# The first norm's root taken out of the input of a two-block transformer kernel and put into what reads the projections

## The chip, the cores and the metric

The kernel runs on one core of one Trainium2 chip. The metric is the device time of one execution in microseconds (us). Several executions of the kernel before gave 969.68, 969.88 and 971.83 us, median 969.88. One more execution was recorded by the hardware profiler; it took 969.85 us.

The engines are named as the profile names them: PE is TensorE (PEld its weight loads), DVE VectorE, ACT ScalarE, POOL GpSimd, SP SyncE, which only issues DMAs here.

## The reference, cut to what matters

Two transformer blocks over 256 tokens of width 1024, all in float32. The change touches only the first norm of the first block and the readers of its product:

```python
u = rms_norm(h, ln_pre_mix)          # h * rsqrt(mean(h*h) + eps) * gain, one root per token
proj = u @ w_in                      # 1024 x 9232
q_a, k_a, v_a, qkv_b, z_b, b_b, a_b, gate_a, gate_b = split(proj)
qa, ka = apply_rope(q_a, cos, sin), apply_rope(k_a, cos, sin)
y_a = attention(qa, ka, v_a)
qkv_b = silu(causal_depthwise_conv(qkv_b, conv_w))    # 4 taps along the tokens
... b_b, a_b -> rates of the gated delta rule; z_b -> silu(z); gate_a, gate_b -> sigmoid
```

The root of a token is one factor on its whole row of `proj`, so it can be applied to `u` before the product or to each part of `proj` after it.

## The kernel before, in words

**Weights.** All weights stream through one pipeline in units of 128 x 1024 floats (512 KB). SP issues the DMA of unit n into one of four raw buffers, once the low half of unit n-4 is made (L478 to L482). ACT rounds the unit to fp32r, the high half `w_hi` (`split_up_to`, L1320 to L1334), into one of six slots; unit n can be rounded only when PE has released the unit that held the slot before (`w_used`), so unit 6 needs unit 0 released. POOL computes the low half `w_lo = raw - w_hi` in two instructions of 128 x 512 per unit (L499 to L505). Each product is three fp32r matmuls: high x high, high x low, low x high. ACT's roundings stand in program order among its other work: at most so many units ahead as the calls of `split_up_to` name.

**The input, step `u`.** x lands in two halves of 128 tokens. ACT squares each half with a running sum; DVE makes the root of each in six one-element instructions (`rsqrt_one`); ACT and DVE scale the half by its root into `xn0`; PE transposes it (L947) in fp32 into the banks Q0 to Q3; ACT (odd banks) and DVE (even banks) evict with the gain of each channel as scale into `uH` (fp32r), and DVE then forms `uL = x*gain - uH`. Dummy matmuls (`warm`) keep PE busy until then. The transpose of the convolution taps and gains (`cwr`) is copied by DVE to `cw`.

**The first convolution group, `first_conv` (L900).** For each of the four units (0 to 3): eight matmuls high x high, eight with `uL`. Then for each unit eight matmuls with `w_lo`, at the end of each the unit is released. So the first unit is released only after the whole first part.

**Order after that.** Every engine walks the same list of steps: `u`, `conv 0 0`, `ba`, `conv 0 1`, `rates`, `tri 0`, `conv 0 2`, `decay 0`, (`moba 0 0` inside it), `tok 0` and so on; then a second group of heads with the same steps. For `conv`, DVE runs the taps from the banks: per tile of 128 channels one TENSOR_SCALAR and three SCALAR_TENSOR_TENSOR of 128 x 256, four tiles per step. `rates` is a chain of tiny instructions between DVE and ACT. `tri` gives the products `trg` (mask times decay rates), which PE needs in `decay` (L999). At the end of `decay` DVE adds the masks ("decay log", L2150). PE waits in `tok` for the banks read by the taps of `conv 0 2` (the filling step `moba 0 1` uses L0 and L1) and for the second "decay log" before it transposes into Q0 (L983). The columns of `moba`, `z`, `ga`, `gb` are filling steps: their matmuls stand between the latency-bound parts of PE's list.

**The root helpers.** `rsqrt_one` (L1933) works on one column; its other factors are pointer scalars, so no instruction has two tensor inputs. `rsqrt` (L1921) works on several columns: one TENSOR_SCALAR, then three rounds of three instructions, each with two tensor inputs. Its argument `bank` puts one of these tensors in PSUM; all calls before give it.

Of the kernel before, what the change touches and what calls it, by code (L numbers as in the profile page):

```python
# [22 lines left out]
F32 = mybir.dt.float32  # L23
# [196 lines left out]
def build(nc, a, out, known):  # L220
# [30 lines left out]
    with ctx:  # L251
# [20 lines left out]
        small = place("small", [P, 960])  # L272
# [106 lines left out]
        def tiny(n):  # L379
            free[0] += n  # L380
            assert free[0] <= 960
            return small[:, free[0] - n:free[0]]
# [37 lines left out]
        r1, floor = tiny(8), tiny(8)  # L420
        baH = big("baH", 36, [P, KD, 16], F32R)
# [90 lines left out]
        def _(pe):  # L512
# [387 lines left out]
            def first_conv():  # L900
# [3 lines left out]
                for j in range(4):  # L904
# [27 lines left out]
            for step in SCHEDULE:  # L932
                kind = step[0]
                if kind == "u":
                    n = CONV * 24 + KD
                    pe.wait_ge(*VE(step, "constant"))
                    warm(15)
                    pe.wait_ge(landed["ident"], 16)
                    pe.wait_ge(landed["cwr"], 16)
                    pe.wait_ge(landed["ln0"], 16)  # L940
                    turn(L[3][:, 0:n], cwr[0:n, :], ident[0:n, 0:n]).then_inc(*PE.mark(step, "taps"))
                    warm(5)
                    for t in range(NT):
                        for j in range(4):
                            pe.wait_ge(*(VE(step, "scaled", 1, j) if t == 1 and j < 2 else AC(step, "scaled", t, j // 2)))
                            for i in range(2):
                                last = turn(Q[j][:, i * SEQ + t * P:i * SEQ + (t + 1) * P], xn0[:, t, (2 * j + i) * P:(2 * j + i + 1) * P], ident)  # L947
                            if t == 1:
                                last.then_inc(*PE.mark(step, "turned", j))
                elif step in INSIDE:  # L950
# [363 lines left out]
        def _(act):  # L1314
# [154 lines left out]
            for step in SCHEDULE:  # L1469
# [5 lines left out]
                if kind == "u":  # L1475
# [7 lines left out]
                    load("table", table[:, P:], a["table"][:, P:])  # L1483
                    act.wait_ge(*VE(step, "root", 0))
                    for half in range(2):
                        cc = slice(half * 512, (half + 1) * 512)
# [1030 lines left out]
```

## Time and profile before

| | |
|---|---|
| median of 3 executions | 969.88 us |
| profiled execution | 969.85 us |
| its span, first to last instruction | 968.0 us |
| mean granted TensorE clock | 0.998 |
| PE busy | 958.0 us, 99% |
| POOL busy | 742.8 us, 77% |
| ACT busy | 511.5 us, 53% |
| DVE busy | 365.8 us, 38% |

The profiled execution's own time lies 1.85 us over its span. A share near 100% says that an engine is nearly always occupied; the share of the others is an average over stretches in which they wait and stretches in which they work without a gap, so the timeline of a stretch has to be read as well.

### The profile page before, as it was taken

The page shows a single profiled execution, that of the slowest core. Times are in us where ns is not written, and L with a number is a line of the kernel's source. Part 1 is how long each engine was busy: PE and PEld are TensorE (multiplying, and loading weights), DVE is VectorE, ACT ScalarE, POOL GpSimd, SP SyncE. Part 2 cuts the span into 40 slices and gives each one's busy share as a digit, 9 for nine tenths or more (in the row PEclk, how much of TensorE's full clock was granted, in tenths as well). Part 3 has the DMA queues.
Part 4 walks back from the last instruction along what each step waited for, and adds up shares of the span by engine and source line. Part 5 has one row for each costly group of instructions (what it writes and reads, how often), then busy time and mean ns, then how long its engine had stood idle before and what let it go on. Part 6 is the DMA issues. An engine that isn't in the chain of part 4 may idle for free.

```text
span 968.0 us, 14697 instructions
## 1 busy us (share of the span) xinstructions
PE 958.0 (99%) x5708; PEld 815.1 (84%) x5708; DVE 365.8 (38%) x844; ACT 511.5 (53%) x753; POOL 742.8 (77%) x593
## 2 busy tenths in 40 slices
PE   9999999999999999999999999999999999999997
PEld 8988879988878888888888887899888888888885
DVE  5687625785624245031122245052343241111103
ACT  6576635464644347455354556584566564444431
POOL 5967654876654988899877987778876889888890
PEclk9999999999999999999999999999999999999999
DMA  7746242654434766767644665656565557666541
GB/s 261 216 132 196 89 137 77 181 154 149 132 110 137 255 213 179 237 193 211 202 153 139 211 219 168 233 155 187 182 196 152 152 163 228 182 189 192 179 130 44
DMA packets 76750, 167.33 MB, mean 173 GB/s; under 512 B 8348, under 2 KB 13704, under 8 KB 76552
## 3 DMA queue, kind: packets, MB, share of 16 engines
q1 hardware_dynamic: 71296, 156.40, 53.3%
q10 hardware_dynamic: 5384, 9.99, 3.2%
q8 instruction: 45, 0.74, 0.3%
q14 instruction: 25, 0.20, 0.1%
HBM read 165.32 MB, written 1.05 MB: 172 GB/s over the span
## 4 chain that ended last, share of the span: by engine, by line
PE 97%; DVE 1%; ACT 1%; DMA 0%; issue 0%; DVEq 0%; ACTq 0%
PE L L517 23%; PE L L519 22%; PE L L518 22%; PE Q L519 2%; PE Q L517 2%; PE Q L518 2%; PE L L889 2%; PE L L891 2%; PE L L890 2%; PE Q L734 1%; PE Q L1185 1%; PE L L788 1%; PE L L790 1%; PE L L789 1%; PE Q L852 1%; PE L L827 1%
## 5 line engine op out<-in xcount | busy, mean ns | idle before, releaser
L504 POOL TENSOR_TENSOR w_lo<-raw,w_hi 128x512 fp32r<-128x512 f32 x588 | 741.3, 1299 | 201.7 <-ACT w_hi L1333 201.1
L1333 ACT CAST w_hi<-raw 128x1024 fp32r<-128x1024 f32 x294 | 305.2, 1055 | 244.1 <-PE L L519 106.2
L517 PE MATMUL L<-w_hi,uH 128*128 128x512 f32 (+1 forms) x768 | 305.4, 398 | 0.3
L519 PE MATMUL L<-w_hi,uL 128*128 128x512 f32 (+1 forms) x768 | 296.6, 386 | 0.0
L518 PE MATMUL L<-w_lo,uH 128*128 128x512 f32 (+1 forms) x768 | 296.1, 386 | 0.0
L519 PEld LDWEIGHTS L<-w_hi,uL 128*128 128x128 f32 x768 | 144.3, 188 | 29.8
L517 PEld LDWEIGHTS L<-w_hi,uH 128*128 128x128 f32 x768 | 144.5, 188 | 29.3 <-DVE uL L1949 1.5
L518 PEld LDWEIGHTS L<-w_lo,uH 128*128 128x128 f32 x768 | 144.7, 188 | 26.5 <-issue 0.5
L517 PE MATMUL L<-w_hi,hH 128*128 128x512 f32 x176 | 69.0, 392 | 0.0
L519 PE MATMUL L<-w_hi,hL 128*128 128x512 f32 x176 | 68.6, 390 | 0.0
L518 PE MATMUL L<-w_lo,hH 128*128 128x512 f32 x176 | 68.5, 389 | 0.0
L1910 DVE TENSOR_TENSOR hL<-Q,hH 128x512 fp32r<-128x512 f32 x22 | 15.2, 691 | 123.5 <-ACT hH L1766 123.1
L1916 DVE TENSOR_SCALAR small<-small 128x1 f32<-128x1 f32 (+1 forms) x177 | 39.0, 220 | 25.6 <-ACT xv L1683 13.1
L1983 DVE TENSOR_TENSOR L<-L,gA 128x512 f32<-128x512 f32 x19 | 13.3, 699 | 90.7 <-ACT hg L1424 90.2
L1949 DVE TENSOR_TENSOR uL<-Q,uH 128x512 fp32r<-128x512 f32 x28 | 19.3, 691 | 53.1 <-ACT uH L1345 52.8
L1919 DVE SCALAR_TENSOR_TENSOR hm<-L,small,sil 128x512 f32<-128x512 f32 x20 | 15.0, 750 | 63.4 <-PE L L519 63.1
L519 PEld LDWEIGHTS L<-w_hi,hL 128*128 128x128 f32 x176 | 33.0, 188 | 7.0
L517 PEld LDWEIGHTS L<-w_hi,hH 128*128 128x128 f32 x176 | 33.1, 188 | 6.7
L518 PEld LDWEIGHTS L<-w_lo,hH 128*128 128x128 f32 x176 | 33.1, 188 | 6.6
L889 PE MATMUL L<-uH,w_hi 128*128 128x256 f32 x128 | 36.5, 285 | 0.0
L891 PE MATMUL L<-uH,w_lo 128*128 128x256 f32 x128 | 36.2, 283 | 0.0
L890 PE MATMUL L<-uL,w_hi 128*128 128x256 f32 x128 | 36.2, 283 | 0.0
(367 smaller groups left out, 1288.3 us busy)
## 6 DMA issues: line engine op xcount, KB each, us to landing
raw<-in_w_in SPq DMA_DIRECT2D x88, 512.0 KB, 3.7
raw<-in_w_ffn_gate SPq DMA_DIRECT2D x22, 512.0 KB, 3.7
raw<-in_w_ffn_up SPq DMA_DIRECT2D x22, 512.0 KB, 3.6
raw<-in_w_ffn_down SPq DMA_DIRECT2D x22, 512.0 KB, 3.6
raw<-in_w_gate SPq DMA_DIRECT2D x22, 512.0 KB, 3.7
raw<-in_w_up SPq DMA_DIRECT2D x22, 512.0 KB, 3.7
raw<-in_w_down SPq DMA_DIRECT2D x22, 512.0 KB, 3.5
raw<-in_w_out SPq DMA_DIRECT2D x16, 512.0 KB, 3.6
```

The lines of the kernel that those rows point to most:

```text
L504: last = nc.gpsimd.tensor_tensor(lo[:, cc], raw[:, n % RAW, cc], hi[:, cc].bitcast(F32), ALU.subtract)
L517: mm(dst, sH, wH, start=start, stop=False)
L518: mm(dst, sH, wL, start=False, stop=False)
L519: return mm(dst, sL, wH, start=False, stop=stop)
L889: mm(bank, sH, uH[:, k, :], start=k == 0, stop=False)
L890: mm(bank, sH, uL[:, k, :], start=False, stop=False)
L891: last = mm(bank, sL, uH[:, k, :], start=False, stop=k == KD - 1)
L1333: copy(halves[SLOT[u]][0], raw[:, u % RAW, :]).then_inc(w_hi_there, 1)
L1910: v(V.tensor_tensor(out_, x_, y_, op), *name)
L1916: v(V.tensor_scalar(out_, x_, s1, s2_, op0, op1), *name)
L1919: v(V.scalar_tensor_tensor(out=out_, in0=x_, scalar=s_, in1=y_, op0=op0, op1=op1), *name)
L1949: vector_next(V.tensor_tensor(uL[:, 4 * half:4 * half + 4, t * P:(t + 1) * P], heads(Q[2 * t + half]), uH[:, 4 * half:4 * half + 4, t * P: ...
```

## The change

The root no longer stands between x and the transposes. PE transposes x itself as each half lands; `uH` and `uL` are then gain times x, without the root. The root is applied later:

- DVE makes both roots after its last `uL`, with `rsqrt` on two columns and no `bank`, and multiplies the identity with each root (`diag0`, two instructions of 128 x 128). PE multiplies a matrix of ones with `diag0`: in bank Q1 every partition then holds the root of each token as a row. DVE copies it to `rows0` (128 x 256).
- PE waits for "diagonal" between the `uL` products and the `w_lo` products of `first_conv`.
- DVE multiplies the banks of each convolution step by `rows0` before the taps: four times 128 x 256 in the first, two times 128 x 512 in the other five; and `baT` by it.
- `tri 0`: DVE multiplies the rotation tables `cos1` and `sin1` in place by the roots, four TENSOR_SCALAR of 128 x 128, ahead of `trg`.
- ACT's evictions of v, z, ga, gb take the root as their scale.
- POOL makes only the first half of the low half of unit 3; DVE makes the second ("last low") after the diagonal; the DMA of unit 7, and PE's last unit of `first_conv`, wait for it.
- The table's DMA (740 KB) is issued after ACT's evictions of `uH`; `warm(15)` and `warm(5)` become `warm(7)`.

```diff
+        rows0 = tiny(SEQ)
+        diag0 = big("diag0", 60, [P, NT, P])
@@ SP
+                if n == 3 + RAW:
+                    sp.wait_ge(*VE(("u",), "last low"))
@@ POOL
-                for half in range(2):
+                for half in range(1 if n == 3 else 2):
@@ PE, first_conv
+                pe.wait_ge(*VE(("u",), "diagonal"))
+                for t in range(NT):
+                    last = mm(Q[1][:, t * P:(t + 1) * P], C[:, 0, 0:P], diag0[:, t, :], start=True, stop=True)
+                last.then_inc(*PE.mark(("u",), "rows"))
                 for j in range(4):
                     wH, wL = unit(n0 + j, 2)
                     pe.wait_ge(w_lo_there, n0 + j + 1)
+                    if j == 3:
+                        pe.wait_ge(*VE(("u",), "last low"))
@@ PE, step u
-                    warm(15)
+                    warm(7)
                     pe.wait_ge(landed["ident"], 16)
...
-                    warm(5)
                     for t in range(NT):
+                        pe.wait_ge(landed[f"x{t}"], 16)
                         for j in range(4):
-                            pe.wait_ge(*(VE(step, "scaled", 1, j) if t == 1 and j < 2 else AC(step, "scaled", t, j // 2)))
                             for i in range(2):
-                                last = turn(Q[j]..., xn0[:, t, ...], ident)
+                                last = turn(Q[j]..., x0[:, t, ...], ident)
@@ ACT
-                    load("table", table[:, P:], a["table"][:, P:])
-                    act.wait_ge(*VE(step, "root", 0))
-                    ... (three scalings of xn0)
                     split_up_to(1)
+                    act.wait_ge(*VE(step, "taps"))
                     for j in (1, 3):
                         ... (evictions to uH, roundings)
+                    load("table", table[:, P:], a["table"][:, P:])
@@ DVE, step u
-                    (roots by rsqrt_one as the sums arrive, two scalings of xn0)
                     ... (uH and uL)
+                    dve.wait_ge(*AC(step, "ss", 1))
+                    ts(rv[:, 0:NT], ss[:, 0:NT], 1.0 / D, EPS, ALU.mult, ALU.add)
+                    rsqrt(rstd0, rv[:, 0:NT])
+                    for t in range(NT):
+                        ts(diag0[:, t, :], ident, rstd0[:, t:t + 1], None, ALU.mult, None, *((step, "diagonal") if t else ()))
+                    dve.wait_ge(w_hi_there, 4)
+                    hi, lo = halves[SLOT[3]]
+                    tt(lo[:, UNIT // 2:], raw[:, 3, UNIT // 2:], hi[:, UNIT // 2:].bitcast(F32), ALU.subtract, step, "last low")
+                    dve.wait_ge(*PE(step, "rows"))
+                    v(V.tensor_copy(rows0, Q[1][:, 0:SEQ]))
@@ DVE, conv
+                        if (gr, part) == (0, 0):
+                            tt(src, src, rows0, ALU.mult)
+                        elif ct % 2 == 0:
+                            both = ... (the whole bank, two tiles)
+                            tt(both, both, each(rows0, 2), ALU.mult)
@@ DVE, tri
                         dve.wait_ge(landed["table"], 16)
+                        for t in range(NT):
+                            ts(cos1[:, t, :], cos1[:, t, :], rstd0[:, t:t + 1], None, ALU.mult, None)
+                            ts(sin1[:, t, :], sin1[:, t, :], rstd0[:, t:t + 1], None, ALU.mult, None)
```

## Rows read from the trace of the kernel before

**Rows 1.** The page, first part: busy time and share of each engine.
```profile
PE 958.0 (99%) x5708; PEld 815.1 (84%) x5708; DVE 365.8 (38%) x844; ACT 511.5 (53%) x753; POOL 742.8 (77%) x593
```

**Rows 2.** Timeline of the start: start us, length us, engine, line, operation, [idle before].
```profile
1.32 5.53 PE L898 MATMUL Q<-C 128*128 128x128 f32 x30 [1.32 <-DVE C L2049]
...
6.79 1.30 PE L898 MATMUL Q<-C 128*128 128x128 f32 x10
...
6.37 1.06 ACT L1482 ACTIVATE xn<-x 128x1024 f32<-128x1024 f32 x1 [0.58 <-DMA x<-in_x]
...
8.89 1.03 ACT L1333 CAST w_hi<-raw 128x1024 fp32r<-128x1024 f32 x1
...
10.00 22.83 POOL L504 TENSOR_TENSOR w_lo<-raw,w_hi 128x512 fp32r<-128x512 f32 x18 [9.56 <-ACT w_hi L1333]
...
11.28 1.19 PE L910 MATMUL L<-uH,w_hi 128*128 128x256 f32 x8
...
14.31 2.04 DVE L1919 SCALAR_TENSOR_TENSOR uL<-Q,small,uH 128x256 fp32r<-128x256 f32 x4
...
19.03 4.00 PE L920 MATMUL L<-uH,w_lo 128*128 128x256 f32 x32
```

**Rows 3.** Timeline of PE in a narrow stretch: where `ba` begins.
```profile
22.87 0.28 PE L956 MATMUL Q<-uH,baH 128*16 128x256 f32 x1
```

**Rows 4.** One window: length, busy (instructions) of PE, PEld, DVE, ACT, POOL, clock, DMA.
```profile
3.00:4.00 1.00, 1.00 (x6) 1.00 (x6) 0.00 (x0) 0.77 (x2) 0.00 (x0) 1.00 0.97 353
```

**Rows 5.** Timeline of DVE and POOL, instructions on SBUF operands, around 106, 16 and 10 us.
```profile
105.91 5.10 DVE L2199 TENSOR_TENSOR Td<-AT,table 64x256 f32<-64x256 f32 x4
...
105.14 8.69 POOL L504 TENSOR_TENSOR w_lo<-raw,w_hi 128x512 fp32r<-128x512 f32 x6 [4.78 <-ACT w_hi L1333]
...
16.38 0.23 DVE L2074 CAST baH<-small 128x128 fp32r<-128x128 f32 x1
16.64 1.27 DVE L1910 TENSOR_TENSOR baL<-small,baH 128x128 fp32r<-128x128 f32 x1
...
16.46 2.60 POOL L504 TENSOR_TENSOR w_lo<-raw,w_hi 128x512 fp32r<-128x512 f32 x2
...
9.70 0.61 DVE L2059 TENSOR_SCALAR xn<-x,small 128x256 f32<-128x256 f32 x2
...
10.00 1.44 POOL L504 TENSOR_TENSOR w_lo<-raw,w_hi 128x512 fp32r<-128x512 f32 x1 [9.56 <-ACT w_hi L1333]
```

**Rows 6.** Groups of DVE by form: busy us, mean ns.
```profile
L1910 DVE TENSOR_TENSOR Q<-Q,small 128x512 f32<-128x512 f32 x12 | 8.4, 699 | 0.4
...
L1910 DVE TENSOR_TENSOR small<-small,Q 128x4 f32<-128x4 f32 x12 | 1.9, 158 | 0.4
```

**Rows 7.** Timeline of ACT, DVE and POOL from `rates` to the end of `decay`.
```profile
47.34 0.22 ACT L1501 ACTIVATE small<-small 128x16 f32<-128x16 f32 x1
...
49.26 0.40 DVE L1914 TENSOR_SCALAR Q<-Q 128x16 f32<-128x16 f32 x2 [2.75 <-ACT Q L1505]
...
51.61 1.41 DVE L1910 TENSOR_TENSOR trg<-table,Q 128x512 f32<-128x512 f32 x2
...
51.66 7.52 POOL L504 TENSOR_TENSOR w_lo<-raw,w_hi 128x512 fp32r<-128x512 f32 x6 [3.01 <-ACT w_hi L1333]
...
63.93 0.69 DVE L1910 TENSOR_TENSOR Dm<-Q,table 128x512 f32<-128x512 f32 x1
```

**Rows 8.** Timeline of PE: the products of `trg`, and the first transposes of `tok 0`.
```profile
54.87 1.96 PE L999 MATMUL Q<-trg,table 128*128 128x512 f32 x4
...
64.89 1.48 PE L983 MATMUL Q<-table,C 128*128 128x128 f32 x12
```

**Rows 9.** The same places in the second group of heads: DVE, then PE.
```profile
190.45 0.48 DVE L1914 TENSOR_SCALAR C<-L,small 128x256 f32<-128x256 f32 x1 [1.25 <-PE L L891]
...
201.33 0.69 DVE L1910 TENSOR_TENSOR Dm<-Q,table 128x512 f32<-128x512 f32 x1
...
206.03 1.47 PE L983 MATMUL Q<-table,C 128*128 128x128 f32 x12
```

More of the change, by code:

```diff
@@ L271, in build @@
         table = place("table", [P, 5 * P + 2 * NT * HD + ROPE2 + LEVELS * HALF])
-        small = place("small", [P, 960])
+        small = place("small", [P, 960 + SEQ])
         at[0] += (base - at[0]) % SPAN
@@ L380, in tiny @@
             free[0] += n
-            assert free[0] <= 960
+            assert free[0] <= 960 + SEQ
             return small[:, free[0] - n:free[0]]
@@ L936, in _ @@
                     pe.wait_ge(*VE(step, "constant"))
[L937 removed]
+                    warm(7)
                     pe.wait_ge(landed["ident"], 16)
[L939 to L942 removed]
                     for t in range(NT):
+                        pe.wait_ge(landed[f"x{t}"], 16)
                         for j in range(4):
[L945 removed]
                             for i in range(2):
[L947 removed]
+                                last = turn(Q[j][:, i * SEQ + t * P:i * SEQ + (t + 1) * P], x0[:, t, (2 * j + i) * P:(2 * j + i + 1) * P], ident)
                             if t == 1:
                                 last.then_inc(*PE.mark(step, "turned", j))
+                        if t == 0:
+                            pe.wait_ge(landed["cwr"], 16)
+                            pe.wait_ge(landed["ln0"], 16)
+                            turn(L[3][:, 0:n], cwr[0:n, :], ident[0:n, 0:n]).then_inc(*PE.mark(step, "taps"))
                 elif step in INSIDE:
@@ L1482, in _ @@
                         actf(xn0[:, t, :], x0[:, t, :], ACT.Square, accum_out=ss[:, t:t + 1]).then_inc(*AC.mark(step, "ss", t))
-                    load("table", table[:, P:], a["table"][:, P:])
-                    act.wait_ge(*VE(step, "root", 0))
-                    for half in range(2):
-                        cc = slice(half * 512, (half + 1) * 512)
-                        actf(xn0[:, 0, cc], x0[:, 0, cc], ACT.Copy, scale=rstd0[:, 0:1]).then_inc(*AC.mark(step, "scaled", 0, half))
                     split_up_to(1)
-                    act.wait_ge(*VE(step, "root", 1))
-                    actf(xn0[:, 1, 512:D], x0[:, 1, 512:D], ACT.Copy, scale=rstd0[:, 1:2]).then_inc(*AC.mark(step, "scaled", 1, 1))
+                    act.wait_ge(*VE(step, "taps"))
                     for j in (1, 3):
@@ L1560, in _ @@
                             act.wait_ge(*PE(("att", 0), "out", 1))
+                        act.wait_ge(*VE(("u",), "diagonal"))
                         for t in range(NT):
-                            copy(mtok[:, 2, t, :, :], L[2 + t][:].rearrange("p (h d) -> p h d", h=GH)).then_inc(*AC.mark(step, "v", t))
+                            actf(mtok[:, 2, t, :, :], L[2 + t][:].rearrange("p (h d) -> p h d", h=GH), ACT.Copy, scale=rstd0[:, t:t + 1]).then_inc(*AC.mark(step, "v", t))
                 elif kind == "feat":
@@ L1605, in _ @@
                     for t in range(NT):
-                        last = actf(dst[:, t, c * 512:(c + 1) * 512], L[banks[t]][:], fn)
+                        last = actf(dst[:, t, c * 512:(c + 1) * 512], L[banks[t]][:], fn, scale=rstd0[:, t:t + 1])
                     last.then_inc(*AC.mark(step))
@@ L2049, in _ @@
                     v(V.memset(C[:, 0, :], 1.0), step, "constant")
-                    for t in range(NT):
-                        dve.wait_ge(*AC(step, "ss", t))
-                        ts(rv[:, t:t + 1], ss[:, t:t + 1], 1.0 / D, EPS, ALU.mult, ALU.add)
-                        rsqrt_one(rstd0[:, t:t + 1], rv[:, t:t + 1], step, "root", t)
-                        if t == 0:
-                            dve.wait_ge(*PE(step, "taps"))
-                            v(V.tensor_copy(cw, L[3][:, 0:CONV * 24 + KD]), step, "taps")
-                    for j in range(2):
-                        cc = slice(j * SEQ, (j + 1) * SEQ)
-                        vector_next(V.tensor_scalar(xn0[:, 1, cc], x0[:, 1, cc], rstd0[:, 1:2], None, ALU.mult), step, "scaled", 1, j)
+                    dve.wait_ge(*PE(step, "taps"))
+                    v(V.tensor_copy(cw, L[3][:, 0:CONV * 24 + KD]), step, "taps")
                     for j in range(4):
@@ L2077, in _ @@
                     dve.wait_ge(*PE(step))
-                    v(V.tensor_copy(baT[0:16, :], Q[0][0:16, 0:SEQ]), step, "turned")
+                    tt(baT[0:16, :], Q[0][0:16, 0:SEQ], rows0[0:16, :], ALU.mult, step, "turned")
                 elif kind == "rates":
@@ L2104, in _ @@
                         dst = C[:, part * GH + ct, :]
+                        if (gr, part) == (0, 0):
+                            tt(src, src, rows0, ALU.mult)
+                        elif ct % 2 == 0:
+                            both = (Q[2 + ct // 2] if (gr, part) == (0, 1) else L[2 * (part % 2) + ct // 2])[:].rearrange("p (a n) -> p a n", a=2)
+                            tt(both, both, each(rows0, 2), ALU.mult)
                         ts(dst, src, cwv[:, 3, tile:tile + 1], None, ALU.mult, None)
```

6 lines of the change are left out of this document (3 added, 3 removed).

## The prediction

> **What bounds the kernel now.** I read the page first: PE is busy 99% of the span, everything else at most 77% [rows 1]. So the time is PE's work plus PE's idle time, and this change takes almost nothing from PE's work. What it can gain is the start, before PE has real work; what it can lose is any place where PE waits anew. I therefore went to the timeline of the start and to the places where DVE, which gets all the new work, stands closely ahead of PE.
>
> At the start PE turns dummy products from 1.32, and the first product of the model starts at 11.28 us. From there PE runs without a gap: eight blocks of eight products, then 32 products with `w_lo` from 19.03, then `ba` at 22.87 [rows 2, 3]. A product of 256 columns costs 0.12 us (4.00 us less a tail of 0.16, over 32). POOL starts at 10.00 and has no gap in 18 instructions, 1.27 us each.
>
> The profiled execution took 969.85 us, its span 968.0; the sum below is made on 969.85, which is 0.03 under the median of the runs, so nothing has to be carried over.
>
> **Part one, the start: what goes.** The roots, the scalings and the dummy products were all ahead of 11.28. x's second half is there at 6.37 and its square ends at about 7.5 [rows 2]; ACT then rounds unit 0 (1.03 us), which ends at about 8.7. The transposes of x are done by then (second half landed 6.37, eight transposes, about 1.3 us). So the first product starts at 8.7, 2.6 us earlier, and PE reaches the new wait, after eight blocks of 0.96, at 16.4.
>
> **Part one: what comes.** The wait is for "diagonal". ACT's order gives DVE's last `uL`: rounding to 8.7, two evictions to 9.5, two roundings to 11.6, two evictions to 12.5, then DVE's last pair of `uL`, at 0.51 each [rows 2], to 13.6. There DVE begins 13 instructions: one TENSOR_SCALAR for the mean, ten of `rsqrt`, two for the diagonal. Without trouble they cost eleven times 0.16 to 0.2 (the 158 ns row, and its gaps) and two times about 0.27, so 2.8 us: diagonal at 16.4, no wait at all.
>
> But none of them has an operand in PSUM, and POOL works without a gap. What that means is in [rows 5]: four DVE instructions of 64 x 256 whose inputs both lie in SBUF took 5.10 us, 1.27 each, while POOL beside them slowed from 1.27 (22.83 over 18 [rows 2]) to 1.45 (8.69 over 6). They take turns: one DVE instruction per POOL instruction. The subtraction `baL`, only 128 columns, took 1.27 too. So length does not matter; a DVE instruction of this kind ends shortly after POOL's current one. Nine of the 13 (the three rounds in `rsqrt`) have two SBUF inputs. The other four have one; the TENSOR_SCALAR of `xn` is of that kind, and POOL's first instruction, begun at 10.00 while `xn` ran to 10.31, took 1.44 instead of 1.27, so that kind seems to hold the same resource. The bounds for one small instruction are 0.16 [rows 6] and 1.41 (1.27 plus gap and turn); I take 1.3, as `baL` is nearest.
>
> How long is POOL busy? It starts at 8.7 and can go on through units 0 to 5: that is 11 instructions (unit 3 has one now), 14.0 us, and about 0.5 for the turns: to 23.2. Unit 6 needs the slot of unit 0, which PE releases only behind the new wait, so there POOL stops. From 13.6 to 23.2 DVE gets about 7 to 8 of its instructions through; the other five or six then cost 0.2 to 0.3 each, 1.0 in all. Diagonal: 24.2. (If the DMAs of units 4 and 5, issued at 11.3 and 13.9, are late, POOL has a gap and DVE catches up inside it; POOL's end then moves by as much. The result stays within 1 us.)
>
> PE resumes at 24.2, makes the two row products (0.45) and the 32 products with `w_lo` (3.84): `ba` begins at 28.5 instead of 22.87, **plus 5.6**. "last low" (0.7 to 1.6) ends before PE's fourth unit at 27.5; the copy of the rows and `baL` end before 28.5; unit 7's DMA, held to 25, is split by about 33, and PE needs it at 36. These hide.
>
> One more term. PE has then stood for 7.8 us. After its first standing, at 1.32, it took 5.53 us for 30 dummy instructions, while ten of them took 1.30 later [rows 2]; less a tail of 0.17 that is 0.113 each, so thirty would take 3.6, and 1.9 us were lost. The window 3 to 4 shows a granted clock of 1.00, but only six instructions in flight [rows 4]: that pace is the lower level, 1.2 GHz and not 2.4. Bounds: nothing, or the 1.9 us again. I take 1.9, the only row there is. The trace has no later idle time of PE over 0.9 us that would test it. The Trainium skill (TensorE: Matmul & The Clock Gate, Part 1) says that TensorE is at 1.2 GHz after standing idle and rises to 2.4 once it is busy; at the start the trace agrees (the 1.9 us), in the middle of the run no row shows it. With the rule the sum is 982.9, without it 981.0.
>
> **Part two, from `rates` to `tok 0`.** Here DVE has no slack. It ends the second "decay log" at 64.62, and PE needs it at 64.89 [rows 7, 8]: 0.3 us. The new work on this path:
>
> - two bank multiplications in `conv 0 1`, 0.70 plus 0.03 gap each [rows 6], 1.46. They hide: `rates` begins 1.46 later, but ACT's sigmoid, which reads its first result, has a table load in front of it and runs only at 47.34, and DVE waited 2.75 us for ACT behind it [rows 7].
> - four TENSOR_SCALAR on the rotation tables, in SBUF, where `tri` begins, at about 51.4, ahead of `trg` at 51.61. POOL's six instructions begin at 51.66 [rows 7]. The first costs 0.3, the other three meet POOL: 1.35 each if they take turns as in [rows 5]; sum 4.35. If they do not, 0.27 each as the cast `baH` (0.23), sum 1.1. Bounds 1.1 and 5.6.
> - two bank multiplications in `conv 0 2`, 1.46, exposed.
>
> The TENSOR_SCALAR is the open point, since `baH` (0.23, one SBUF input) ran from 16.38 to 16.61 just as POOL changed from one instruction to the next at 16.46, which decides nothing. I take the turns, by POOL's 1.44. The Trainium skill (SBUF — State Buffer, Who interferes with whom) says that two SBUF inputs against a GpSimd read, and also a tensor_scalar in its two-port mode, take the shared port pair for a whole instruction. For two inputs the trace agrees (1.27); for one input no row settles it. By the rule the sum is 982.9, by the cast's row 979.7.
>
> PE first waits at `trg` (ready 56.7, wanted 54.87), then for the banks of `conv 0 2`, then for "decay log": 64.62 + 4.35 + 1.46 = 70.43 against 64.89. All three waits together are the last one: **plus 5.5**.
>
> **Part three, all other edits.** In the second group the same additions, 1.46 per step, meet an idle time of 1.25 in front of `conv 1 2`, so decay log ends at about 203.7 instead of 202.02, and PE comes at 206.03 [rows 9]: hidden; were that slack gone, it would cost 1.7. `conv 0 0`: four times 0.47 are 1.9 us, before an idle time of 5.5 of DVE: hidden. Scales in ACT's evictions: the engine is 53% busy and the instructions stay the same in number: nothing. The table's DMA, issued at about 13.6 and 7.4 us under way before, is wanted at 51. POOL's saved instruction (1.27) only helps a queue that waits for PE's release.
>
> **Sum.** 969.85 + 5.6 + 1.9 + 5.5 = 982.85, forecast **982.9 us**.
>
> **Rivals.**
>
> *The tables do not meet POOL* (a one-input instruction passes freely). Then part two costs 64.62 + 1.1 + 1.46 - 64.89 = 2.3, and the diagonal hardly moves, since POOL's end sets it: 979.7. For it `baH` at 0.23, against it POOL's 1.44.
>
> *Small instructions slip in more often than once per POOL instruction.* No row shows two-input instructions under 128 columns beside POOL. If DVE gets two or three per POOL instruction, the diagonal comes at about 19: PE goes on to 23.3, plus 0.4, too short for the clock, and part two 5.5: 975.8.
>
> *The start is won (the other side).* If neither kind waits for POOL, the diagonal is at 16.4, PE's `ba` begins at 16.4 + 4.3 = 20.7, 2.2 us early, and part two costs its 2.3: 969.9, no change. It decides at the diagonal: before 16.4 the start is won. With part two's cover better by a us (ACT's chain or a shorter multiplication) it is faster, 968. For it: the sum of the durations alone. Against it: the 1.27 of `baL`, which is an instruction of the same shape at the same place.
>
> **How the numbers follow.** Forecast 0.50, its own range 980.5 to 985.5 (the clock's 1.9 away, or paid at the waits of part two as well). Tables free: 0.20. Slipping in: 0.13. Start won: 0.17, of which faster by over 0.2% 0.06, within 0.2% 0.09 and slower 0.02. 0.2% (1.9 us) is about what a measurement of this kernel tells from no change. So faster 0.06, same 0.09, slower 0.85. The range 972.5 to 985.5 takes in the first three and leaves out the last: 0.8.
>
> **What would show it.** The first product at about 8.7; DVE instructions of `rsqrt` of 1.2 to 1.4 us each from 13.6 to 23, and short ones after; a wait of PE for DVE `diag0` of 7 to 8 us; products twice as long for some us after it; POOL idle from 23 until PE releases unit 0; the table multiplications 1.3 us each; PE waits of some 2 us at L999 and 3 to 4 us in `tok 0`. It is wrong if the `rsqrt` instructions take 0.2 us while POOL is busy, or if PE passes `tok 0` without waiting.

## The result, and the profile after

The kernel after takes **984.38 us** (median of four executions, 982.99 to 985.77); the kernel before, run beside it, 970.82 (969.68 to 971.83). The ratio is 1.014, with a 95% interval of 1.0116 to 1.0164. The forecast was 982.9, in the range 972.5 to 985.5. The profiled execution of after took 985.53 us (span 983.7, mean granted clock 0.990), 15.7 us more than that of before; it is one of the two upper executions of the four (985.5 and 985.8, clock 0.990; the others 983.0 and 983.2, clock 0.994).

The page of after, first part, answers to [rows 1]: PE has 961.4 us of busy time in a span of 983.7, so it stands for 22.3 us, where before it stood for 10.0. Its busy time is 3.4 us longer, too, with 22 matmuls fewer: 12.3 us more standing and 3.4 more work are the 15.7 of the span.

```profile
PE 961.4 (98%) x5686; PEld 817.2 (83%) x5686; DVE 384.9 (39%) x861; ACT 510.9 (52%) x750; POOL 741.1 (75%) x592
```

The view of PE's waits names where (line, what it waited for, us in total, times, longest):

```profile
PE Q L921 <- DVE diag L1920: 6.8, 1, 6.8
PE L L521 <- issue: 3.1, 1, 3.1
PE Q L1009 <- DVE trg L1916: 1.5, 1, 1.5
...
PE Q L1147 <- ACT vn L1635: 1.2, 1, 1.2
```

Two new places carry nearly everything: the diagonal at the start, and DVE ahead of `tok 0` (1.5 and 3.1). For the stand of 3.1 this view names no releaser ("issue"); PE goes on at 74.74, 0.10 us behind the end of DVE's last tap of `conv 0 2`, and the same place in e13_short_stands is put down to DVE. The timeline of PE at the start answers to [rows 2, 3]. The first product starts at 8.72 instead of 11.28, the eighth block ends at 16.66, and then PE stands until 23.50:

```profile
8.72 1.22 PE L914 MATMUL L<-uH,w_hi 128*128 128x256 f32 x8 [1.03 <-ACT w_hi L1343]
...
15.54 1.12 PE L918 MATMUL L<-uL,w_hi 128*128 128x256 f32 x8
23.50 1.23 PE L921 MATMUL Q<-diag,C 128*128 128x128 f32 x4 [6.85 <-DVE diag L1920]
24.38 6.33 PE L930 MATMUL L<-uH,w_lo 128*128 128x256 f32 x32
30.55 0.28 PE L966 MATMUL Q<-uH,baH 128*16 128x256 f32 x1
```

The 32 products with `w_lo` take 6.33 us where they took 4.00, and `ba` begins at 30.55, 7.7 us later than before. The windows of after (length; busy of PE, PEld, DVE, ACT, POOL; clock; DMA) say why:

```profile
26.00:28.00 2.00, 2.00 (x12) 2.00 (x11) 0.00 (x0) 1.04 (x1) 0.35 (x1) 0.50 1.02 353
...
30.00:32.00 2.00, 2.00 (x20) 1.75 (x19) 1.11 (x3) 1.87 (x2) 2.00 (x3) 1.00 0.32 77
...
75.00:77.00 2.00, 2.00 (x5) 1.54 (x5) 1.90 (x4) 1.98 (x3) 0.26 (x1) 0.50 0.01 4
...
81.00:83.00 2.00, 2.00 (x14) 1.79 (x13) 1.90 (x4) 1.97 (x5) 2.00 (x3) 1.00 0.58 200
```

The granted clock falls while PE stands (0.66 from 19 to 20, 0.50 from 20 on), is still 0.50, that is 1.2 GHz, in the products behind the stand of 6.8 us, and is 1.00 again from 30. It is at 0.50 a second time behind the stand of 3.1 us in `tok 0`, from 74 to about 80.8.

What kept the diagonal is in the timelines of DVE and of POOL. Of the first two DVE instructions shown, the TENSOR_SCALAR for the mean takes 0.43 and the first one of `rsqrt`, with one SBUF input, 1.22:

```profile
13.41 1.68 DVE L1922 TENSOR_SCALAR small<-small 128x2 f32<-128x2 f32 x2
15.12 1.21 DVE L1925 SCALAR_TENSOR_TENSOR small<-small 128x2 f32<-128x2 f32 x1
16.37 1.19 DVE L1916 TENSOR_TENSOR small<-small 128x2 f32<-128x2 f32 x1
17.59 2.40 DVE L1925 SCALAR_TENSOR_TENSOR small<-small 128x2 f32<-128x2 f32 x2
20.03 0.16 DVE L1916 TENSOR_TENSOR small<-small 128x2 f32<-128x2 f32 x1
...
21.01 2.44 DVE L1920 TENSOR_SCALAR diag<-table,small 128x128 f32<-128x128 f32 x2
```

```profile
8.74 11.24 POOL L508 TENSOR_TENSOR w_lo<-raw,w_hi 128x512 fp32r<-128x512 f32 x9 [8.30 <-ACT w_hi L1343]
20.89 2.48 POOL L508 TENSOR_TENSOR w_lo<-raw,w_hi 128x512 fp32r<-128x512 f32 x2 [0.91 <-ACT w_hi L1343]
```

The next four instructions, with two elements in each partition and two SBUF inputs, take 1.2 us each, as long as one instruction of POOL (11.24 over 9 is 1.25). From 19.98 to 20.89 POOL waits for a rounding, and in that gap the same kind takes 0.16 to 0.18; when POOL is back, the two halves of the diagonal take 1.22 each.

Last, DVE and PE on the way to `tok 0`, answering to [rows 7, 8]:

```profile
59.10 4.13 DVE L1920 TENSOR_SCALAR table<-table,small 128x128 f32<-128x128 f32 x4
...
77.26 0.69 DVE L1916 TENSOR_TENSOR Dm<-Q,table 128x512 f32<-128x512 f32 x1
```

```profile
64.22 1.98 PE L1009 MATMUL Q<-trg,table 128*128 128x512 f32 x4 [1.53 <-DVE trg L1916]
...
74.74 0.77 PE L521 MATMUL L<-w_hi,uH 128*128 128x512 f32 x1 [3.06 <-issue]
75.31 0.63 PE L522 MATMUL L<-w_lo,uH 128*128 128x512 f32 x1
75.73 0.63 PE L523 MATMUL L<-w_hi,uL 128*128 128x512 f32 x1
...
80.00 1.85 PE L993 MATMUL Q<-table,C 128*128 128x128 f32 x12
```

The masks are added at 77.95, but the transposes start at 80.00: the products of PE's filling step in front of them run at nearly half their pace (0.43 us apart, 0.23 at full clock). The transposes are 15.1 us later than before [rows 8]; 0.57 us of the 15.68 are left for everything behind them.

### The profile page after: what moved, and what is told of

Its sections match the earlier page's. It is cut to its first block, busy times and chain, and to the rows that moved or that the text cites. A ratio compares the mean times of both kernels' runs of the same rounds, so it can differ in the third digit from the quotient of the medians.

```text
span 983.7 us, 14672 instructions
## 1 busy us (share of the span) xinstructions
PE 961.4 (98%) x5686; PEld 817.2 (83%) x5686; DVE 384.9 (39%) x861; ACT 510.9 (52%) x750; POOL 741.1 (75%) x592
## 4 chain that ended last, share of the span: by engine, by line
PE 91%; DVE 3%; ACT 2%; DMA 1%; POOL 1%; issue 1%; SPq 0%; DVEq 0%; ACTq 0%
PE L L521 22%; PE L L523 21%; PE L L522 21%; PE Q L523 2%; PE Q L521 2%; PE Q L522 2%; DMA raw<-in_w_in 1%; PE L L895 1%; PE L L894 1%; PE L L893 1%; PE Q L738 1%; POOL w_lo L508 1%; PE Q L1195 1%; PE L L792 1%; PE L L794 1%
## 5 line engine op out<-in xcount | busy, mean ns | idle before, releaser
L1922 DVE TENSOR_SCALAR small<-small 128x1 f32<-128x1 f32 (+2 forms) x165 | 37.7, 228 | 20.6 <-ACT xv L1689 13.1
```

Source lines behind the costliest of these rows:

```text
L1922: v(V.tensor_scalar(out_, x_, s1, s2_, op0, op1), *name)
```

## The experiments

Each ratio is to the kernel before as executed beside that kernel. The medians of before were 970.82 us beside after and 969.79 to 970.69 beside the others, so a difference of two medians given below can be off by about 1 us; where that matters, the difference by the ratios stands with it. A time in a timeline is that of one execution.

### The instructions of the root, with one operand in PSUM (e1_bank)

```diff
-                    rsqrt(rstd0, rv[:, 0:NT])
+                    rsqrt(rstd0, rv[:, 0:NT], bank=Q[3])
```

> Changed kernel, but the root's second tensor lies in PSUM (rsqrt with bank Q3); nothing else. Theory (an instruction with two SBUF inputs waits for POOL's current one): the nine instructions fall from 1.2 us while POOL works to 0.2 us, the two TENSOR_SCALAR ahead of them (1.7 us together) and the two of the diagonal (1.2 us each) stay held. Diagonal at 13.4 + 1.7 + 1.8 + 2.4 = 19.3 instead of 23.4, so PE stands some 3 us instead of 6.8 and the time falls by 3.8 us, to about 980.6; if the shorter stand also leaves PE at full speed, by a further 2.3, to 978.3. Rival (DVE is slow there for another reason, such as many small instructions in a row): the nine stay near 1.2 us and the time stays at 984.4.

Measured: 975.47 us (975.17 to 975.98), ratio 1.0058 (1.0043 to 1.0073), 8.9 us less than after (8.0 by the ratios): more than was expected. DVE and PE in this kernel:

```profile
13.36 0.43 DVE L1922 TENSOR_SCALAR small<-small 128x2 f32<-128x2 f32 x1
13.82 0.16 DVE L1922 TENSOR_SCALAR Q<-small 128x2 int32<-128x2 int32 x1
...
15.76 1.82 DVE L1920 TENSOR_SCALAR diag<-table,small 128x128 f32<-128x128 f32 x2
17.61 1.67 DVE L1916 TENSOR_TENSOR w_lo<-raw,w_hi 128x512 fp32r<-128x512 f32 x1
```

```profile
17.64 0.71 PE L921 MATMUL Q<-diag,C 128*128 128x128 f32 x4 [1.04 <-DVE diag L1920]
18.10 4.07 PE L930 MATMUL L<-uH,w_lo 128*128 128x256 f32 x32
...
22.01 0.28 PE L966 MATMUL Q<-uH,baH 128*16 128x256 f32 x1
```

Ten instructions of `rsqrt` take 1.9 us (13.8 to 15.7) instead of some 6.7 (14.3 to 21.0 in after), POOL working all the while. One tensor moved out of SBUF is the whole edit; it is an input of the nine, and what the first of `rsqrt` writes, which falls from 1.22 to 0.16 as well (the expectation had this one unchanged). Together with the 0.16 that the same instructions took in POOL's gap, this shows that they waited for POOL's use of SBUF and not for one another. PE stands 1.0 us, its clock holds, `ba` is at 22.01, 8.5 us earlier than in after and 0.9 earlier than before. In the profiled execution the rest of the gain is in `tok 0`: the transposes start at 69.45, 10.55 us earlier than in after. The clock falls here behind the stand of 1.5 us at `trg` and is 1.00 again from about 60, so that the products in front of the transposes run at full pace.

### Dummy products in front of the diagonal (e3_dummies)

```diff
+                warm(30)
                 pe.wait_ge(*VE(("u",), "diagonal"))
```

> Changed kernel, with 30 dummy products (0.21 us each, 6.4 us) on PE ahead of its wait for the diagonal; its results are not used. Theory (the stand of 6.8 us puts PE to the lower clock level): the 32 products with the low halves take 4.0 us instead of 6.33, and the time falls by 2.3 us, to 982.1; PE's waits in part two are unchanged. Rival (the slow products come from their operands or from POOL and DVE reading the same slots): they stay at 6.3 us and the time at 984.4 or above.

Measured: 981.86 (981.70 to 981.93), ratio 1.0123 (1.0106 to 1.0140), 2.5 us less than after (1.6 by the ratios, whose intervals overlap; the trace is the firmer evidence). `warm(30)` makes 60 passes; the diagonal comes 0.9 us later than in after. PE:

```profile
17.19 6.86 PE L902 MATMUL Q<-C 128*128 128x128 f32 x60
24.38 0.71 PE L922 MATMUL Q<-diag,C 128*128 128x128 f32 x4 [0.32 <-DVE diag L1921]
24.85 4.07 PE L931 MATMUL L<-uH,w_lo 128*128 128x256 f32 x32
```

The products with `w_lo` are back at 4.07, though they start no earlier, and the clock is 1.00 from 16 to 28. So the stand costs its length and then the lower clock; the second part is 2.3 us on these products (6.33 less 4.07) and 0.4 on the two row products. `ba` is at 28.75, 1.8 us earlier than in after. The other 1.9 us between the two profiled executions lie in `tok 0`, where the clock fell in after and did not fall here (it fell at `trg`).

### Four multiplications alone, in the kernel before (e4_before_tables)

```diff
                         dve.wait_ge(landed["table"], 16)
+                        for t in range(NT):
+                            ts(cos1[:, t, :], cos1[:, t, :], 1.0, None, ALU.mult, None)
+                            ts(sin1[:, t, :], sin1[:, t, :], 1.0, None, ALU.mult, None)
```

> Kernel before, with one part of the change alone: four TENSOR_SCALAR of 128 x 128 on the rotation tables ahead of trg, times the constant 1. Theory (held by POOL, and DVE had 0.3 us of slack): they take about 4.1 us, PE waits for trg and before tok 0, the time rises by 4.1 - 0.3 = 3.8 us to about 974.6, and by up to 2.3 more if PE's stand costs it the clock. Rival (not held): they take 1.1 us, and the time rises by 0.8 us to 971.6.

Measured: 972.78 (972.61 to 973.01), ratio 1.0030 (1.0018 to 1.0042), plus 3.0 us. DVE, then POOL:

```profile
51.19 2.98 DVE L1914 TENSOR_SCALAR table<-table 128x128 f32<-128x128 f32 x4
```

```profile
51.46 7.59 POOL L504 TENSOR_TENSOR w_lo<-raw,w_hi 128x512 fp32r<-128x512 f32 x6 [3.00 <-ACT w_hi L1333]
```

The 2.98 stand in the kernel's time nearly whole: DVE has no slack here, as the prediction said. The expectation had 4.1 for the four, and they take 2.98, though POOL starts 0.27 us behind the first in both kernels. The timelines of single instructions show why. With the factor in the instruction the first takes 0.23 us and the second starts at 51.45, 0.01 ahead of POOL; with the factor read from SBUF, in after, the first takes 0.29 and the second starts 0.06 behind POOL's start at 59.37. The second here, then the second in after, then POOL in after:

```profile
51.45 0.23 DVE L1914 TENSOR_SCALAR table<-table 128x128 f32<-128x128 f32 x1
```

```profile
59.43 1.33 DVE L1920 TENSOR_SCALAR table<-table,small 128x128 f32<-128x128 f32 x1
```

```profile
59.37 7.47 POOL L508 TENSOR_TENSOR w_lo<-raw,w_hi 128x512 fp32r<-128x512 f32 x6 [3.04 <-ACT w_hi L1343]
```

So two instructions went ahead of POOL here and one in after, and each of the others took 1.2 to 1.3 in both. No run moved this start on purpose. PE's stand of 1.6 us in `tok 0` left the clock at 1.00.

### The rotation tables with the root in PSUM (e2b_tables_psum)

```diff
+                        rootP = Q[2][:, 500:500 + NT]
+                        v(V.tensor_copy(rootP, rstd0))
                         for t in range(NT):
-                            ts(cos1[:, t, :], cos1[:, t, :], rstd0[:, t:t + 1], None, ALU.mult, None)
-                            ts(sin1[:, t, :], sin1[:, t, :], rstd0[:, t:t + 1], None, ALU.mult, None)
+                            each_root = rootP[:, t:t + 1].to_broadcast([P, HD])
+                            tt(cos1[:, t, :], cos1[:, t, :], each_root, ALU.mult)
+                            tt(sin1[:, t, :], sin1[:, t, :], each_root, ALU.mult)
```

> Changed kernel, but the four multiplications of the rotation tables are TENSOR_TENSOR with the root read from PSUM (one small copy more), at the same place. Theory (a one-input SBUF instruction is held by POOL, one with its other input in PSUM is not): the four and the copy take 1.5 us instead of 4.13, PE does not wait at the products of trg, and comes about 2.7 us too early before tok 0 in place of 5.4, too short for the clock: the place costs 2.7 us where it cost 7.4, the time falls by 4.7 us to 979.7. If the clock falls all the same, by 2.6 only, to 981.8. Rival (their 1 us each is their own length, whatever POOL does): the four stay near 4 us and the time at 984.4.

Measured: 981.59 (980.41 to 982.23), ratio 1.0110 (1.0096 to 1.0124), 2.8 us less than after (2.9 by the ratios). DVE:

```profile
59.34 1.25 DVE L1916 TENSOR_TENSOR table<-table,Q 128x128 f32<-128x128 f32 x4
```

The four fall from 4.13 to 1.25 us, 0.31 each, beside the same work of POOL. The first of the four in after, ahead of POOL, took 0.29 in its old form, so it is not the new form that is faster: the one-input instructions of this size from SBUF to SBUF did wait for POOL, and the rival "the tables do not meet POOL" is out. The gain in the medians is about that difference: PE still stands for 2.1 us in `tok 0`, its clock falls behind that stand too, and the transposes start at 76.51, 1.2 us behind the masks. At the start PE stood for 7.0 us, about as long as in after, and the products with `w_lo` took 5.42 and not 6.33.

### Root, diagonal and tables all over PSUM (e5_all_psum)

The two edits above together, and the diagonal made in the same way:

```diff
-                        ts(diag0[:, t, :], ident, rstd0[:, t:t + 1], None, ALU.mult, None, ...)
+                        tt(diag0[:, t, :], ident, rootP[:, t:t + 1].to_broadcast([P, P]), ALU.mult, ...)
```

> Changed kernel with all root arithmetic out of POOL's way: rsqrt with its bank in PSUM, the diagonal and the rotation tables by TENSOR_TENSOR with the root from PSUM, nothing moved. Theory: the diagonal is ready at about 16.4, PE hardly waits, ba begins at 20.8 instead of 22.87 in the kernel before (minus 2.1 us); from rates to tok 0 DVE has 1.5 + 1.46 us more than before and 0.3 of slack (plus 2.6 us). Sum: 970.3, within 0.1% of the kernel before. Rival (the four places where PE waited also cost it the clock, whatever their length): up to 2.3 us more, 972.6.

Measured: 972.05 (971.54 to 972.76, 11 executions), ratio 1.0015 (1.0006 to 1.0023). PE has no wait for the diagonal left, and `ba` begins at 21.27, 1.6 us earlier than before. One window (columns as above) shows the clock behind the stand of 2.1 us that remains in `tok 0`:

```profile
65.00:67.00 2.00, 2.00 (x6) 1.54 (x6) 1.86 (x5) 1.99 (x5) 2.00 (x2) 0.50 0.00 0
```

Even with all waits for POOL gone, the change is not a gain: what is left is DVE's work itself, 1.25 for the tables, 0.2 for the copy of the root, 1.46 for the banks of `conv 0 2`, and 1.2 for the clock, less the 1.6 us that the start gains and the 0.3 of slack.

### Without the multiplications of `conv 0 2` (e7_no_conv02)

```diff
-                        elif ct % 2 == 0:
+                        elif ct % 2 == 0 and (gr, part) != (0, 2):
```

> As e5, with the two bank multiplications of conv 0 2 left out (one third of the first group's convolution channels then lacks the root). Theory: DVE is bound there, so the full 1.46 us come back: 968.8. Rival (PE waits for the banks or for ACT there, not for DVE's length): the time stays at e5's.

Measured: 970.32 (969.95 to 973.90, 10 executions), ratio 1.0003 (0.9993 to 1.0014), 1.7 us less than e5_all_psum. In its result a third of the first group's convolution channels lacks the root. The two intervals overlap, so the term of 1.46 is borne out but not measured closely. In the trace PE's stand in `tok 0` is 0.6 us instead of 2.1 and the clock is 1.00 from 50 to 72, so that some of the clock's 1.2 should be in the difference too.

### The work moved to where DVE waits (e6_moved)

From e5_all_psum: the tables are multiplied in `ba`, behind `baT`, and the two banks of `conv 0 2` inside `rates`, while DVE waits for ACT's ln:

```diff
                     ts(a_, a_, 0.0, None, ALU.max, None)
+                    dve.wait_ge(*fed(("conv", 0, 2)))
+                    for b in range(2):
+                        both = L[b][:].rearrange("p (a n) -> p a n", a=2)
+                        tt(both, both, each(rows0, 2), ALU.mult)
                     dve.wait_ge(*AC(step, "ln"))
```

> As e5, with the two places moved out of DVE's bound stretch: the rotation tables are multiplied in the step ba, where DVE stood for 3.7 to 5.5 us, and both banks of conv 0 2 are multiplied in rates, while DVE waits 1.1 us for ACT's logarithm. Theory: of the 2.6 us that e5 pays from rates to tok 0 about 0.1 to 0.4 stay, the 2.1 us won at the start are kept: 968.0, 0.2% under the kernel before. Rival (what the start wins is given back by the weight pipeline, because POOL or the DMAs have not moved with PE): no faster than 969.8.

Measured: **969.03** (968.75 to 970.85, 11 executions), ratio 0.9986 (0.9977 to 0.9995): faster than before by 0.14% by the ratio (0.9 us by the medians), and the only complete version whose interval lies below 1. Three of its waits of PE, and two rows of PE's timeline:

```profile
PE Q L1147 <- ACT vn L1635: 1.2, 1, 1.2
PE L L914 <- ACT w_hi L1343: 1.0, 1, 1.0
PE Q L993 <- ACT tok L1535: 0.2, 1, 0.2
```

```profile
17.08 4.07 PE L930 MATMUL L<-uH,w_lo 128*128 128x256 f32 x32
...
63.21 1.53 PE L993 MATMUL Q<-table,C 128*128 128x128 f32 x12
```

The start is won by 1.95 us [rows 2], 1.7 of it is still there at the transposes [rows 8], and 1.0 in the span (967.0 against 968.0). The clock is 1.00 from 50 to 72.

### Without the scale in the evictions of z, ga and gb (e8_no_scales)

From e6_moved:

```diff
-  actf(dst[...], L[banks[t]][:], fn, scale=rstd0[:, t:t + 1])
+  actf(dst[...], L[banks[t]][:], fn)
```

> As e6, with the root left out of ACT's evictions of z, ga and gb (these lack the root then). In e6 such an eviction pair takes 1.26 us where it took 1.09 without the scale from SBUF, and in front of the first scan two pairs stand between PE's last filling product and the copy that PE waits for (PE waits 1.22 us there, 0.86 in the kernel before). Theory (ACT is bound there): minus 0.35 us against e6, 968.7. Rival (ACT is 53% busy, its length is hidden): the time of e6, 969.0.

Measured: 968.74 (968.36 to 969.91, 11 executions), ratio 0.9986 (0.9977 to 0.9995), 0.3 us below e6_moved, a difference that the executions do not resolve. The traces do: the pair of evictions takes 1.27 us in after and 1.09 here, and PE's wait for ACT's `vn` behind them is 0.9 instead of 1.2. ACT in after, then in this kernel:

```profile
130.17 1.27 ACT L1612 ACTIVATE z<-L,small 128x512 f32<-128x512 f32 x2
```

```profile
114.09 1.09 ACT L1612 ACTIVATE z<-L 128x512 f32<-128x512 f32 x2
```

### POOL makes both halves of unit 3 (e9_pool_both)

From e6_moved, with "last low" and its waits gone:

```diff
-                for half in range(1 if n == 3 else 2):
+                for half in range(2):
```

> As e6, with one part of the change undone: POOL makes both halves of the low half of unit 3 again, DVE none, and neither the DMA of unit 7 nor PE waits for DVE's. Theory (with the start 1.9 us earlier POOL, at 1.27 us per instruction without a gap, is nearly the bound for units 6 and 7 in conv 0 1): POOL comes about 0.9 us late there and the time rises by 0.5 to 0.9 us, to 969.5 to 969.9. Rival (POOL has slack; the only effect is that DVE and POOL share the work): no change, 969.0.

Measured: 969.55 (968.94 to 970.74, 11 executions), ratio 0.9996 (0.9987 to 1.0004), 0.5 us above e6_moved (1.0 by the ratios); the two intervals overlap. POOL then works without a gap from 8.85 to 44.09, where in e6_moved it had gaps. That "last low" is worth something, as expected, is likely but not shown.

### Shorter stands before `tok 0`: two tries (e11_dummies_tok, e12_psum_dummies)

The second fall of the clock was so far only read in traces. Dummy products in front of the wait in `tok 0`, 20 in after, 14 in e5_all_psum:

```diff
                             pe.wait_ge(*AC(("conv", gr, part), "silu"))
+                            if b == 0 and gr == 0:
+                                for i in range(20):
+                                    mm(Q[2][:, 0:P], ones, tri, start=True, stop=True)
```

> After, with 20 dummy matmuls of 128 columns on PE between the first part's silu and the wait in tok 0 for the banks of conv 0 2; the wait itself stays, DVE's work is untouched. The profiled kernel after stood 3.1 us there and then had a granted clock of 0.50 from 74.7 to about 80.5. Theory (the second fall of the clock, about 2 us, is what the sum lacked): 20 dummies of 0.113 fill 2.3 us, the stand is 0.8, the clock stays at 1.00, and the first transposes of tok 0 come at 78.0, when the last mask addition is made, not at 80.0; the profiled time falls from 985.5 to 983.4, and the executions no longer spread over 983 to 986 but lie at 983.0 to 983.5. Rival (the 2 us come from the later banks themselves, the clock only happens to be low while PE would wait for the masks anyway): no change, 984.4 as the median of after.

> The version with root, diagonal and rotation tables over PSUM (972.05), with 14 such dummy matmuls at the same place. There PE stood 2.1 us and the clock was at 0.50 from about 64 to 67.3, the first transposes of tok 0 at 67.19 although the last mask was added at 65.99. Theory (the fall of the clock is exposed by 1.2): 14 dummies leave 0.5 us of standing, clock 1.00, transposes at 66.0 to 66.2, 970.9 to 971.1. Rival (the place is bound by DVE's masks alone): no change, 972.0.

Measured: 984.54 (983.13 to 984.69), ratio 1.0138 (1.0124 to 1.0152), and 971.62 (971.33 to 974.74), ratio 1.0014 (1.0005 to 1.0023): neither can be told from its base. Both had a wrong price: each dummy is two passes, and 20 of them took 4.62 us, 14 of them 3.29, longer than the stands of 3.1 and 2.1 that they should shorten. PE in e11_dummies_tok, from the start and from part two:

```profile
24.70 4.97 PE L930 MATMUL L<-uH,w_lo 128*128 128x256 f32 x32
...
63.17 2.71 PE L1012 MATMUL Q<-trg,table 128*128 128x512 f32 x4 [1.52 <-DVE trg L1919]
72.11 4.62 PE L988 MATMUL Q<-table 128*128 128x128 f32 x40
79.32 1.47 PE L996 MATMUL Q<-table,C 128*128 128x128 f32 x12
```

In this execution the clock also fell earlier, behind the stand of 1.5 us at `trg` (0.50 from 65 to 67). There it costs nothing as far as a stand follows that it can shorten. At the start the same stand as in after, 6.9 us, was followed by products that took 4.97 and not 6.33. In e12_psum_dummies the clock is 1.00 throughout, and the transposes start at 66.16, 0.45 us behind the masks, where e5_all_psum had 1.20.

### Shorter stands, with the right price (e13_short_stands)

After, with 4 dummies before the wait for `trg` (shown) and 10 in front of `tok 0`, placed as the 20 of e11_dummies_tok:

```diff
+                    if gr == 0:
+                        for i in range(4):
+                            mm(Q[0][:, 0:P], ones, tri, start=True, stop=True)
```

> After, with 4 dummy matmuls on PE before the wait for trg and 10 before the wait in tok 0, each of two passes and 0.227 us (20 of them took 4.62 in the run before this one): 0.9 of the stand of 1.5 and 2.3 of the stand of 3.1 are filled, so neither is lengthened; the stand of 6.8 for the diagonal stays. Theory (the second fall of the clock costs after about 2 us at tok 0, where it comes there, and nothing where it comes at trg, since the time is then taken from the next stand): the granted clock stays at 1.00 from 60 to 85; the first transposes of tok 0 start within 0.4 of the end of the last mask addition (after: 77.95 and 80.00); all executions lie with the lower ones of after, 982.4 to 983.5, none at 985.5. Rival (the spread of 983 to 986 is not the second fall but something else, the start for example): the clock is 1.00 there and executions of 985 and more are still seen, the median stays at 984.4.

Measured: 983.41 (981.48 to 984.67), ratio 1.0133 (1.0114 to 1.0152). PE:

```profile
64.28 1.99 PE L1015 MATMUL Q<-trg,table 128*128 128x512 f32 x4 [0.53 <-DVE trg L1922]
...
74.75 0.50 PE L521 MATMUL L<-w_hi,uH 128*128 128x512 f32 x1 [0.77 <-DVE C L1931]
...
78.06 1.53 PE L996 MATMUL Q<-table,C 128*128 128x128 f32 x12 [0.26 <-DVE Dm L1922]
```

This profiled execution goes beside that of after up to 74.7 (first instruction behind the wait at 74.74 and 74.75). There the clock stays at 1.00, and the transposes start at 78.06, at once behind the masks, and not at 80.00. The span is 981.9 against 983.7. So in this pair of traces the second fall costs 1.9 us. In the medians the difference is 1.0 (0.7 by the ratios) and the intervals overlap, so the executions do not show it. Nor did they gather as expected, between 982.4 and 983.5: they lie between 981.48 and 984.67. The rival had some at 985 and more. Neither came, and what spreads them is not explained.

## Why the prediction was right, and what it missed

| step of the prediction | forecast | measured |
|---|---|---|
| first product | 8.7 | 8.72 |
| DVE begins the root | 13.6 | 13.41 |
| diagonal made | 24.2 | 23.45 |
| start, without the clock | +5.6 | +4.9 |
| clock behind the stand | +1.9 | +2.8 (1.4 to 2.8 in four traces) |
| four table products | 4.35 | 4.13 |
| part two, to the masks | +5.5 | +5.4 (e13_short_stands) |
| clock in `tok 0` | 0 | +1.9 to 2.0 |
| scales in ACT's evictions | 0 | +0.3 |
| sum, against the profiled execution | +13.05 | +15.68 |

The measured split of the start: `ba` moved by 7.68; the lower clock cost 2.33 on the 32 products and 0.43 on the row products (0.88 instead of 0.46); the rest is 4.9. Part two in e13_short_stands: 78.06 less 64.89, less 7.74 for the start (`ba` at 30.61 there). In after the same is 7.4, of which 2.0 is the clock.

**The mechanism was right.** One instruction of DVE per instruction of POOL, for those with two SBUF inputs: 1.2 us each, with 2 elements in a partition as with the 128 of `baL`. The row of `baL` [rows 5] was the right one to take, and e1_bank shows it by moving one tensor to PSUM. One-input instructions wait, too: those of 128x128 beside POOL took 1.2 to 1.3, nearly the 1.35 taken, and the one ahead of POOL 0.29; of the two of 128x2 one took 0.43 and one 1.22, where 1.3 each was taken. POOL's 1.44 in [rows 5] had pointed to it and the cast `baH` had not.

**What made the start shorter than forecast** was the gap of 0.91 us of POOL at 19.98, which the prediction named as a possibility, within 1 us: five instructions of DVE passed in it, at 0.16 to 0.18. The diagonal still ended behind POOL's last instruction, 23.45 against 23.37, as the prediction had it.

**The step that was mis-sized is the clock.** The prediction had one fall of the clock, priced at 1.9 by the row of the start [rows 2]. It cost 2.8 in the profiled execution of after; behind the same stand of 6.9 to 7.0 us the 32 products took 6.21 in e13_short_stands, 5.42 in e2b_tables_psum and 4.97 in e11_dummies_tok, which with the row products is a loss of 2.6, 1.8 and 1.4. So 1.9 was a fair price, and no single one fits. The miss is in part two: its stands were priced at their length alone, though the prediction's own range spoke of a fall there. The rival "slipping in" also took a stand of 2.6 us as too short for the clock, and stands of 2.1 were enough. The clock is shown by e3_dummies for the first place and by one pair of traces, after and e13_short_stands, for the second. The Trainium skill (TensorE: Matmul & The Clock Gate, Part 1) says that the engine is at 1.2 GHz after standing idle; here the trace agrees in the middle of the run, with 0.50 granted behind stands of 6.8, 3.1 and 2.1 us. Behind the stand of 1.5 at `trg` it fell in e1_bank, e3_dummies and e11_dummies_tok and not in the profiled execution of after. The prediction read the lower level at the kernel's own start from the pace; the granted clock of [rows 4] is 1.00 there, so no row names the level at that place.

**A term that was missed:** "the instructions stay the same in number: nothing". The eviction with a scale read from SBUF takes 684 ns where the one without takes 594, and a pair of them stands before `vn`, for which PE waits. The Trainium skill (ScalarE: Activation LUTs, What ACT_TABLE_LOAD costs) gives about 93 ns for each operand of one value per partition; the trace agrees with 90.

**What was luck.** At the start two misses cancel in the profiled execution: 0.7 too much for the stand, 0.9 too little for the clock, together 7.5 against 7.7. Part two has no such partner, and the sum is 2.6 short of that execution. The medians of after and of the before beside it differ by 13.6, nearer to the 13.05 of the sum, because the median of after lies between two pairs of executions 2.5 us apart; the lower pair, at 983.0 and 983.2, has no trace.

**Hidden, as forecast:** the additions in `conv 0 1` (DVE's wait for ACT in `rates` shrank from 2.75 to 1.31), the additions of the second group (no wait of PE there), the four of `conv 0 0`, the table's later DMA. About 0.3 us behind the transposes are assigned to nothing.

**The rivals.** "The tables do not meet POOL" falls by e2b_tables_psum. "Slipping in" falls by the 1.2 us of the instructions beside POOL; they slip only where POOL waits. "The start is won" did not come, but e5_all_psum and e6_moved show what it would be: once the chain of the root no longer waits for POOL, the diagonal is there when PE needs it, and the start gains 1.7 to 1.95 us. Only with the moved work on top did the change become a gain of 0.14%; the moved work without the PSUM operands was not run.

## What to carry to other kernels

Before tiny instructions are put between SBUF tiles on DVE, look at what POOL does in that stretch: beside a POOL that never pauses each one with two SBUF inputs costs a POOL instruction (1.2 us here, 0.16 with one operand in PSUM), and a chain of ten took 6.7 us instead of 1.9. Moving a factor from one place to many readers moves work to the engines of the readers, so for each reader find the wait that could take it; the table and bank multiplications cost 2.7 us in front of a waiting PE (e5_all_psum) and at most 0.3 in gaps that DVE had anyway (e6_moved). And price a stand of PE by its length and by the slower products behind it (1.4 to 2.8 us behind the long stand here, 1.9 behind the second), or fill it with dummies whose passes have been counted.

## What the runs showed that was not expected

The clock fell at both stands of 2.1 us that a trace shows, at none of those of 1.6 and 1.4 in `tok 0` (e4_before_tables, e1_bank, e3_dummies), and at those of 1.5 at `trg` in some traces and not in another, in kernels that are the same at that place. How long the products behind a stand stay slow is not fixed either, as the four traces with the stand of 6.9 to 7.0 us show.

The executions of after lie in two pairs, 2.5 us apart, with mean clocks of 0.990 and 0.994. A fall of the clock that comes in one pair and not in the other would fit, but only one execution has a trace, and the four executions of before beside it lie in two pairs 2 us apart as well. So the cause of these pairs stays open.

Four multiplications of 128x128 in SBUF took 2.98 us in one kernel and 4.13 in another with POOL starting at the same distance behind the first; 0.07 us in the start of the second decided on which side of POOL's start it fell, and that cost 1.1 us.
